# Adding the residual rows by accumulating DMAs instead of on VectorE in three of four column blocks

## The chip, the cores and the metric

The kernel runs on one core of a Trainium2 chip. The metric is the device time of one execution in microseconds (us). The core has TensorE (PE, matmuls; PEld is its weight load), VectorE (DVE), ScalarE (ACT), GpSimd (POOL) and SyncE (SP), each with a program of its own and an in-order queue; they wait for one another by semaphores. Sixteen DMA engines move data between the device memory (DRAM), where inputs and outputs lie, and the on-chip buffers.

## The reference

One layer of a diffusion backbone on 512 latent tokens of width 2048 with 256 context tokens. Three head groups (a Hyena long convolution, latent attention with 8 heads, pooling) give a mixed row of 2048 values per token; what ends the layer is this:

```python
x_l = x_l + gt * (out_l @ w_out[l])
return rmsnorm(x_l, final_norm_g)
```

`out_l` is the mixed 512x2048 matrix, `w_out` is 2048x2048, `gt` a gate of one row of 2048 values, `x_l` the layer's input x (the residual), and the norm divides each row by the root of its mean square and multiplies by `final_norm_g`. All of it is float32.

## The kernel before

All engines' programs are written out by hand, one function per engine, with semaphores. This case is about the last stage, the output product. Precision is kept by splitting each operand into a rounded high part and a rest: each product is three matmuls (high times high, high times low, low times high).

The output has 4 column blocks b of 512 columns and 4 token tiles tok of 128 rows; each (b, tok) has a PSUM bank, and bank sets alternate with b. The inner dimension is cut into 4 chunks c, so the stage has 16 chunks n = 4b + c. For a chunk:

- SP loads its weights, 1 MB, to one of three places `wo_raw` (`load_out`, L426), when the chunk three earlier is done on PE.
- ACT rounds them to `wo_hi` (`wo_high`, L850), one of two places, so it waits until PE is done with chunk n - 2.
- DVE takes the difference `wo_lo` (`wo_low`, L1417).
- PE waits for `wo_lo` and runs 48 matmuls of 512 columns (`out_part`, L2004), 12 for each token tile. In the last block, chunks 14 and 15 are run tile by tile (c = 2, then c = 3 for tok 0, and so on).

A block b is finished by the following steps for its 4 token tiles. `residual` on DVE multiplies the PSUM bank by the gate row in place (L1424), waits for that, and adds x, which lies in the row buffer `y`, into `y` (L1426). `row_squares` on ACT (L860) squares 512 columns of `y` and sums them per row. POOL multiplies the same columns by the norm's gain (L506). For blocks 0 to 2 the residuals stand on DVE behind `wo_low(4b+5)`, the squares on ACT behind `wo_high(4b+5)` and ahead of `wo_high(4b+6)`. PE lets block 2 begin when block 0's residuals are done, and block 3 when block 1's are, since they share banks.

After block 3 a tail follows for each token tile: residual, square, the row's sum and root, its reciprocal, scaling of the 2048 columns (1024 by ACT, L1012, and 512 each in two DVE instructions, L1611 and L1612), and two stores of 512 KB by SP. ACT and DVE wait there for POOL's gain products of block 2 (`gained`).

SP loads x into the row buffer `y` ahead of the stage: four DMAs of 1 MB (L438) and one of 1 MB for the gain (L439), behind the last attention product. ACT's place around the squares is this:

```python
for n in range(3, 16):
    wo_high(n)
    if n % 4 == 1 and n > 4:
        for tok in range(4):
            row_squares(n // 4 - 1, tok)
```

Of the kernel before, what the change touches and what calls it, by code (L numbers as in the profile page):

```python
# [17 lines left out]
ALU = mybir.AluOpType  # L18
# [3 lines left out]
P = 128  # L22
D = 2048
KT = D // P
L = 512
# [36 lines left out]
def backbone(nc, mem, t, out):  # L62
# [6 lines left out]
    with ExitStack() as ctx:  # L69
# [3 lines left out]
        def sem(name):  # L73
            return ctx.enter_context(nc.semaphore(name))
# [68 lines left out]
        gate_rows_, gain, y_out = at("gate_rows", FREE + 10, D), at("gain", TAB + 10, D), at("y", FREE + 21, 4 * D)  # L143
# [8 lines left out]
        def wa_raw(s):  # L152
            return wa_raw_[:, s * AW:(s + 1) * AW]

        def lane(x, s, n=1024, pitch=1024):
            return x[:, s * pitch:s * pitch + n]
# [72 lines left out]
        def q_square(i):  # L229
# [53 lines left out]
        pool_done, pool_mm, pool_out = sem("pool_done"), sem("pool_mm"), sem("pool_out")  # L283
        rope_step, st_max, st_rec = sem("dve_step_a"), sem("st_max"), sem("st_rec")

        xr_in, gain_in = sem("x_rows_in"), sem("gain_in")
        wo_in = [sem(f"wo_in{s}") for s in range(3)]
        mix_hi, mix_lo, diag_done, gate_mm, gate_out = sem("mix_hi"), sem("mix_lo"), sem("diag_done"), sem("gate_rows_mm"), sem("gate_out")
        wo_hi, wo_lo, wo_mm, mm_done = sem("wo_hi_done"), sem("wo_lo_done"), sem("wo_mm"), sem("wo_bank_mm")
        oscaled, res_done, osq_done, fin_done, stored = (sem("out_scaled"), sem("y_done_o"), sem("sq_done_o"),  # L290
                                                                     sem("fin_done"), sem("stored"))
# [26 lines left out]
        def _(eng):  # L318
# [116 lines left out]
            load_out(3)  # L435
            eng.wait_ge(pv_mm, 8)
            for i in range(4):
                eng.dma_start(y_out[:, i * D:(i + 1) * D], t["x"][i * P:(i + 1) * P, :]).then_inc(xr_in, 16)  # L438
            eng.dma_start(gain[:], t["gain"].to_broadcast([P, D])).then_inc(gain_in, 16)  # L439
            for n in range(4, 16):  # L440
                out_chunk_done(eng, n - 3)
                load_out(n)
# [7 lines left out]
        @block.gpsimd  # L450
        def _(eng):
            steps = [0]

            def link(ins):
                steps[0] += 1
                ins.then_inc(pool_step, 1)
                eng.wait_ge(pool_step, steps[0])

            for j in range(KT):
                s = j % 2  # L460
                eng.wait_ge(wa_hi_done, j + 1)
                if j >= 2:
                    eng.wait_ge(mmA_done, j - 1)
                eng.tensor_tensor(lane(wa_lo, s, AW, AW), wa_raw(s), lane(wa_hi, s, AW, AW), ALU.subtract).then_inc(wa_lo_done, 1)
            for o in range(2):
                for l in range(4):
                    eng.wait_ge(taps_sq, 4 * o + l + 1)
                    a, b = squares[:, 0:L], squares[:, L:2 * L]
                    if l == 0:
                        if o:  # L470
                            eng.wait_ge(norm_mm, 1)
                        eng.tensor_tensor(total, a, b, ALU.add).then_inc(sq_sum, 1)
                    else:
                        link(eng.tensor_tensor(a, a, b, ALU.add))
                        eng.tensor_tensor(total, total, a, ALU.add).then_inc(sq_sum, 1)
                        eng.wait_ge(sq_sum, 4 * o + l + 1)

            eng.wait_ge(rope_in, 80)
            for g in range(4):
                eng.wait_ge(ev_done, 27 + g)  # L480
                half = 1 << g
                x = U[:, (T_POOL + g) * L:(T_POOL + g + 1) * L]
                if g == 0:
                    link(eng.memset(pads[0], 0.0))
                link(eng.tensor_copy(pads[0][:, 8:8 + L], x))
                a, n = pads[0], 528
                for d in range(g + 1):
                    b = pads[1 + d % 2]
                    n -= 1 << d
                    link(eng.tensor_tensor(b[:, 0:n], a[:, 0:n], a[:, (1 << d):(1 << d) + n], ALU.add))  # L490
                    a = b
                s = a[:, 8 - half:8 - half + L]
                link(eng.tensor_tensor(s[:, 0:8], s[:, 0:8], edge[:, 16 * g:16 * g + 8], ALU.mult))
                link(eng.tensor_tensor(s[:, L - 8:L], s[:, L - 8:L], edge[:, 16 * g + 8:16 * g + 16], ALU.mult))
                link(eng.tensor_scalar(s, s, 1.0 / (2 * half), 1.0, ALU.mult, ALU.mult))
                eng.tensor_tensor(x, s, x, ALU.subtract).then_inc(pool_done, 1)
                eng.wait_ge(pool_done, g + 1)


            eng.wait_ge(gain_in, 16)  # L500
            for b in range(3):
                for tok in range(4):
                    n = 4 * b + tok
                    eng.wait_ge(osq_done, n + 1)
                    yy = y_out[:, tok * D + b * L:tok * D + (b + 1) * L]
                    eng.tensor_tensor(yy, yy, gain[:, b * L:(b + 1) * L], ALU.mult).then_inc(gained, 1)  # L506

        @block.scalar
        def _(eng):
# [341 lines left out]

            def row_squares(b, tok):
                n = 4 * b + tok
                eng.wait_ge(res_done, n + 1)
                if n:
                    eng.wait_ge(osq_done, n)
                else:

                    eng.wait_ge(gate_mm, 16)
                eng.activation(out_tmp[:], y_out[:, tok * D + b * L:tok * D + (b + 1) * L], ACT.Square,  # L860
                               accum_out=ss[:, 4 * tok + b:4 * tok + b + 1]).then_inc(osq_done, 1)
# [89 lines left out]
            for n in range(34):  # L951
                p, i = n // 8, n % 8
# [47 lines left out]
# [6 lines that stand above are left out]
                row_squares(3, tok)  # L1006
                eng.wait_ge(row_sum, tok + 1)
                eng.activation(rs[:, 2 * tok:2 * tok + 1], rs[:, 2 * tok:2 * tok + 1], ACT.Sqrt, bias=eps[:, 0:1], scale=1.0 / D).then_inc(root_done, 1)
                eng.wait_ge(row_scale, tok + 1)
                eng.wait_ge(gained, 9 + tok)  # L1010
                yy = y_out[:, tok * D:tok * D + 1024]
                eng.activation(yy, yy, ACT.Copy, scale=rs[:, 2 * tok + 1:2 * tok + 2]).then_inc(fin_act, 1)  # L1012

        @block.vector
        def _(eng):
# [403 lines left out]
            def residual(b, tok):  # L1419
                n = 4 * b + tok  # L1420
                eng.wait_ge(mm_done, n + 1)
                yy = y_out[:, tok * D + b * L:tok * D + (b + 1) * L]
                bank = psum[:, 4 * (b % 2) + tok, :]
                eng.tensor_tensor(bank, bank, gate_rows_[:, b * L:(b + 1) * L], ALU.mult).then_inc(oscaled, 1)  # L1424
                eng.wait_ge(oscaled, n + 1)
                eng.tensor_tensor(yy, bank, yy, ALU.add).then_inc(res_done, 1)  # L1426
# [104 lines left out]
            for n in range(34):  # L1531
                p, i = n // 8, n % 8
# [58 lines left out]
            eng.wait_ge(gate_mm, 16)  # L1591
            eng.tensor_copy(gate_rows_[:].rearrange("p (a b) -> p a b", a=4), psum[:, 4:8, :]).then_inc(gate_out, 1)
            eng.wait_ge(gate_out, 1)
            eng.wait_ge(xr_in, 64)
            for n in range(4, 16):
                wo_low(n)
                if n % 4 == 1 and n > 4:
                    for tok in range(4):
                        residual(n // 4 - 1, tok)
            eng.wait_ge(gain_in, 16)  # L1600
            for tok in range(4):
                residual(3, tok)
                eng.wait_ge(osq_done, 13 + tok)
# [11 lines left out]
        def _(eng):  # L1615
# [392 lines left out]
            def out_chunk(b, c):  # L2008
                for tok in range(4):
                    mm = out_part(b, c, tok)  # L2010
                    if c == 3:
                        mm.then_inc(mm_done, 1)
                if c < 3:
                    mm.then_inc(wo_mm, 1)
# [7 lines left out]
            for n in range(34):  # L2022
                p, i = n // 8, n % 8
# [49 lines left out]
            eng.wait_ge(gate_out, 1)  # L2073
            for b in (1, 2):
                if b == 2:
                    eng.wait_ge(res_done, 4)
                for c in range(4):
                    out_chunk(b, c)
            eng.wait_ge(res_done, 8)
            out_chunk(3, 0)  # L2080
            out_chunk(3, 1)

# [8 lines left out]
def build(nc, t, out):  # L2091
    with ExitStack() as ctx:
        def alloc(name, cols):
            return ctx.enter_context(nc.sbuf_tensor(name, [P, cols], F32))

        mem = {n: alloc(n, c) for n, c in (("par", N_PAR), ("gcol", 16), ("ident", P), ("ones", P), ("eps", 1))}
        base = (nc.sbuf_base + 31) // 32 * 32

        def at(name, tile, cols, dt=F32):

            return nc.alloc_sbuf_tensor_at(name, [P, cols], dt, offset=base + int(tile * 2048))

        mem["at"], mem["UG"], mem["U"] = at, alloc("UG", KT * L), alloc("U", U_COLS)
        backbone(nc, mem, t, out)
# [106 lines left out]
```

## Time and profile before

| | us |
|---|---|
| median of 3 executions | 993.85 (992.87 to 996.38) |
| the profiled execution | 992.26 |
| its span, first to last instruction | 990.5 |
| mean granted TensorE clock | 0.992 of full speed |
| PE busy | 952.0 (96% of the span) |
| DVE busy | 620.5 (63%) |
| ACT busy | 397.6 (40%) |
| POOL busy | 95.9 (10%) |

Each row of the profile names the line of the kernel, the engine, the operation, the output and the inputs with their shapes. A time in a timeline counts from the span's start. In square brackets stands how long the engine was idle ahead of the instruction, and whose instruction ended that. Ends of matmuls are modelled and overlap: their starts tell the pace. The output stage is the last 185 us or so of the span.

### The profile page before, as it was taken

What the parts mean: (1) busy time and instruction counts of PE and PEld (TensorE: products, weight loads), DVE (VectorE), ACT (ScalarE), POOL (GpSimd) and SP (SyncE); (2) the same over time, 40 slices, a digit from 0 to 9 for tenths busy, and PEclk for the clock granted to TensorE, in tenths of its full rate; (3) what the DMA queues carried; (4) which work ended last, traced back from release to release, by engine and by line L of the source; (5) the groups of instructions that cost most, each with busy time, mean ns of one, the idle gap of its engine ahead of it and who ended that gap; (6) DMA issues with size and microseconds to landing.
All of it is one profiled execution on the core that took longest, in us unless ns stands there. A gap on an engine that the chain in (4) does not pass through costs nothing.

```text
span 990.5 us, 12597 instructions
## 1 busy us (share of the span) xinstructions
PE 952.0 (96%) x5074; PEld 788.2 (80%) x5074; DVE 620.5 (63%) x817; ACT 397.6 (40%) x622; POOL 95.9 (10%) x77
## 2 busy tenths in 40 slices
PE   5999998899999999999999999999999999999996
PEld 3677786678888789888888888888888888888875
DVE  2676987777765676736785563767776765413234
ACT  3555665355224433222322422645445451213124
POOL 1222200210002200000003360000000000202020
PEclk9999999989999999999999999999999999999998
DMA  9999922222222222248784223101002126222314
GB/s 369 426 424 390 333 86 75 85 65 65 85 85 85 75 64 65 78 171 297 255 302 144 86 85 128 43 12 43 12 1 85 44 80 260 85 85 91 122 43 170
DMA packets 28550, 136.17 MB, mean 137 GB/s; under 512 B 3563, under 2 KB 4011, under 8 KB 21452
## 3 DMA queue, kind: packets, MB, share of 16 engines
q1 hardware_dynamic: 28060, 135.23, 38.1%
q8 instruction: 40, 0.66, 0.3%
q10 hardware_dynamic: 432, 0.13, 0.1%
q14 instruction: 18, 0.15, 0.0%
HBM read 131.16 MB, written 4.19 MB: 137 GB/s over the span
## 4 chain that ended last, share of the span: by engine, by line
PE 78%; DVE 11%; ACT 4%; DMA 4%; issue 2%; SPq 0%; DVEq 0%; ACTq 0%
PE pp L1698 31%; PE pp L2004 17%; PE pp L1728 17%; PE pp L1645 4%; DMA wa_raw<-in_wa_dram 2%; PE pp L1622 2%; PE pp L1967 2%; PE pp L1649 1%; DVE w_lo L1127 1%; DVE pt_lo L1397 1%; DMA ada_raw<-in_w_ada_dram 1%; PE pp L1959 1%; PE pp L1958 1%; DVE softmax_stats L1382 1%; ACT U L819 0%
## 5 line engine op out<-in xcount | busy, mean ns | idle before, releaser
L1698 PE MATMUL pp<-h_hi,w_hi 128*128 128x512 f32 x544 | 216.0, 397 | 8.2 <-ACT UG L616 6.2
L1698 PE MATMUL pp<-h_lo,w_hi 128*128 128x512 f32 x544 | 213.1, 392 | 0.0
L1698 PE MATMUL pp<-h_hi,w_lo 128*128 128x512 f32 x544 | 212.9, 391 | 0.0
L1127 DVE TENSOR_TENSOR w_lo<-w_raw,w_hi 128x1024 fp32r<-128x1024 f32 x68 | 86.5, 1272 | 101.0 <-ACT w_hi L612 100.7
L612 ACT ACTIVATE w_hi<-w_raw 128x1024 fp32r<-128x1024 f32 x68 | 71.9, 1058 | 171.2 <-PE pp L1698 133.4
L1698 PEld LDWEIGHTS pp<-h_hi,w_hi 128*128 128x128 f32 x544 | 102.9, 189 | 33.5 <-issue 9.1
L1698 PEld LDWEIGHTS pp<-h_hi,w_lo 128*128 128x128 f32 x544 | 102.8, 189 | 22.0
L1698 PEld LDWEIGHTS pp<-h_lo,w_hi 128*128 128x128 f32 x544 | 103.1, 189 | 21.2 <-issue 0.7
L2004 PE MATMUL pp<-wo_hi,m_hi 128*128 128x512 f32 x256 | 100.7, 393 | 1.7 <-DVE wo_lo L1417 1.7
L2004 PE MATMUL pp<-wo_hi,m_lo 128*128 128x512 f32 x256 | 99.6, 389 | 0.0
L2004 PE MATMUL pp<-wo_lo,m_hi 128*128 128x512 f32 x256 | 99.6, 389 | 0.0
L1417 DVE TENSOR_TENSOR wo_lo<-wo_raw,wo_hi 128x2048 fp32r<-128x2048 f32 x16 | 36.7, 2291 | 84.1 <-ACT wo_hi L850 84.0
L850 ACT ACTIVATE wo_hi<-wo_raw 128x2048 fp32r<-128x2048 f32 x16 | 30.6, 1914 | 93.0 <-PE pp L2004 93.0
L2004 PEld LDWEIGHTS pp<-wo_hi,m_hi 128*128 128x128 f32 x256 | 48.1, 188 | 12.4 <-DVE wo_lo L1417 2.1
L2004 PEld LDWEIGHTS pp<-wo_lo,m_hi 128*128 128x128 f32 x256 | 48.1, 188 | 10.2 <-issue 0.5
L2004 PEld LDWEIGHTS pp<-wo_hi,m_lo 128*128 128x128 f32 x256 | 48.1, 188 | 10.1
L506 POOL TENSOR_TENSOR y<-y,gain 128x512 f32<-128x512 f32 x12 | 15.5, 1296 | 345.9 <-ACT out_tmp L860 345.6
L1397 DVE TENSOR_TENSOR pt_lo<-pp,pt_hi 128x768 fp32r<-128x768 f32 x32 | 30.5, 953 | 26.1 <-ACT pt_hi L827 26.0
L827 ACT ACTIVATE pt_hi<-pp 128x768 fp32r<-128x768 f32 x32 | 26.0, 812 | 50.9 <-PE pp L1967 50.9
L1622 PE MATMUL pp<-ada_raw,silu_spread 128*32 128x256 f32 x512 | 33.8, 406 | 8.2 <-DMA ada_raw<-in_w_ada_dram 7.8
L819 ACT ACTIVATE U<-pp,softmax_stats 128x768 f32<-128x768 f32 x32 | 28.9, 903 | 27.8 <-DVE softmax_stats L1384 27.6
L1645 PE MATMUL pp<-a_hi,wa_hi 128*128 128x512 f32 x80 | 35.3, 441 | 2.5 <-DVE a_lo L1031 2.5
(308 smaller groups left out, 1876.3 us busy)
## 6 DMA issues: line engine op xcount, KB each, us to landing
w_raw<-in_wb_dram SPq DMA_DIRECT2D x68, 512.0 KB, 3.6
ada_raw<-in_w_ada_dram SPq DMA_DIRECT2D x15, 2048.0 KB, 12.8
w_gate_raw<-in_w_gate_dram SPq DMA_DIRECT2D x16, 1024.0 KB, 4.9
wo_raw<-in_w_out_dram SPq DMA_DIRECT2D x16, 1024.0 KB, 4.8
wa_raw<-in_wa_dram SPq DMA_DIRECT2D x16, 320.0 KB, 7.6
UG<-in_xT_dram SPq DMA_DIRECT2D x8, 512.0 KB, 8.7
y<-in_x_dram SPq DMA_DIRECT2D x4, 1024.0 KB, 9.3
out_dram<-y SPq DMA_DIRECT2D x8, 512.0 KB, 3.2
```

Source lines behind the costliest of these rows:

```text
L612: eng.activation(lane(wb_hi, n % 2), lane(wb_raw, n % KW), ACT.Copy).then_inc(wb_hi_done, 1)
L819: eng.activation(prob(n % 3).rearrange("p (a b) -> p a b", a=2), psum[:, 2 * (n % 2):2 * (n % 2) + 2, 0:384], ACT.Exp, bias=st[:, 4 * s + ...
L827: eng.activation(pt_hi[:].rearrange("p (k q) -> p k q", k=6)[:, :, o:o + P], psum[:, 4:6, :].rearrange("p a b -> p (a b)")[:, 0:LK].rearra ...
L850: eng.activation(wo_high_[n % 2][:], wo_raw[n % 3][:], ACT.Copy).then_inc(wo_hi, 1)
L1127: eng.tensor_tensor(lane(wb_lo, n % KW), lane(wb_raw, n % KW), lane(wb_hi, n % 2), ALU.subtract).then_inc(wb_lo_done, 1)
L1397: eng.tensor_tensor(lo, psum[:, 4:6, :].rearrange("p a b -> p (a b)")[:, 0:LK].rearrange("p (k q) -> p k q", k=6), hi, ALU.subtract).then_ ...
L1417: eng.tensor_tensor(wo_low_[n % 3][:], wo_raw[n % 3][:], wo_high_[n % 2][:], ALU.subtract).then_inc(wo_lo, 1)
L1622: mm = eng.matmul(ps[7][32 * strip:32 * strip + 32, 0:256], spread[:, 32 * kk:32 * kk + 32], src[:, kk * 256:(kk + 1) * 256], start=kk < 4 ...
L1645: mm = eng.matmul(ps[i][:], w, x, start=first and n == 0, stop=last and n == 2)
L1698: mm = eng.matmul(ps[i][:], w, x, start=(kk == 0 and m == 0), stop=(kk == KT - 1 and m == 2))
L1728: mm = eng.matmul(dst, w, x, start=first and m == 0, stop=last and m == 2)
L2004: mm = eng.matmul(psum[:, 4 * (b % 2) + tok, :], a, v[:, w:w + L], start=(kk == 0 and m == 0), stop=(kk == 15 and m == 2))
```

## The change

In blocks 0 to 2 DVE writes the gated product straight from PSUM to `y` and adds nothing. GpSimd then issues a DMA for each (b, tok) that reads 128x512 values (256 KB) of x from DRAM and adds them onto `y`. These are the first DMAs in POOL's program. ACT's squares of block b wait until all four DMAs of that block have landed (semaphore `xacc_in` at 64b + 64); before, square (b, tok) waited for the add of its own tile. PE lets blocks 2 and 3 begin when the gated products of blocks 0 and 1 are there. SP loads only the last 512 columns of x ahead (4 DMAs of 256 KB in place of 4 of 1 MB), and the loads of x and of the gain share one semaphore. Block 3 keeps its residual on DVE.

```diff
@@ SP
-                eng.dma_start(y_out[:, i * D:(i + 1) * D], t["x"][i * P:(i + 1) * P, :]).then_inc(xr_in, 16)
-            eng.dma_start(gain[:], t["gain"].to_broadcast([P, D])).then_inc(gain_in, 16)
+                eng.dma_start(y_out[:, i * D + 1536:(i + 1) * D], t["x"][i * P:(i + 1) * P, 1536:D]).then_inc(xr_in, 16)
+            eng.dma_start(gain[:], t["gain"].to_broadcast([P, D])).then_inc(xr_in, 16)
@@ POOL
-            eng.wait_ge(gain_in, 16)
+            def residual_rows(b, tok):
+                n = 4 * b + tok
+                eng.wait_ge(oscaled, n + 1)
+                eng.dma_start(y_out[:, tok * D + b * L:tok * D + (b + 1) * L], t["x"][tok * P:(tok + 1) * P, b * L:(b + 1) * L],
+                              accum_op=ALU.add).then_inc(xacc_in, 16)
+
+            for tok in range(4):
+                residual_rows(0, tok)
+            eng.wait_ge(xr_in, 80)
             for b in range(3):
                 for tok in range(4):
                     n = 4 * b + tok
                     eng.wait_ge(osq_done, n + 1)
                     yy = y_out[:, tok * D + b * L:tok * D + (b + 1) * L]
                     eng.tensor_tensor(yy, yy, gain[:, b * L:(b + 1) * L], ALU.mult).then_inc(gained, 1)
+                if b < 2:
+                    for tok in range(4):
+                        residual_rows(b + 1, tok)
@@ ACT, row_squares
-                eng.wait_ge(res_done, n + 1)
+                if b < 3:
+                    eng.wait_ge(xacc_in, 64 * b + 64)
+                else:
+                    eng.wait_ge(res_done, tok + 1)
@@ DVE, residual
+                if b < 3:
+                    eng.tensor_tensor(yy, bank, gate_rows_[:, b * L:(b + 1) * L], ALU.mult).then_inc(oscaled, 1)
+                    return
                 eng.tensor_tensor(bank, bank, gate_rows_[:, b * L:(b + 1) * L], ALU.mult).then_inc(oscaled, 1)
                 eng.wait_ge(oscaled, n + 1)
                 eng.tensor_tensor(yy, bank, yy, ALU.add).then_inc(res_done, 1)
@@ DVE, around the stage
-            eng.wait_ge(xr_in, 64)
...
-            eng.wait_ge(gain_in, 16)
+            eng.wait_ge(xr_in, 80)
@@ PE
                 if b == 2:
-                    eng.wait_ge(res_done, 4)
+                    eng.wait_ge(oscaled, 4)
...
-            eng.wait_ge(res_done, 8)
+            eng.wait_ge(oscaled, 8)
```

Two places show what stands in a row on an engine. In the rows below, the number behind a name (`wo_hi_137`) is a buffer, the semaphores that a row waits for stand in brackets, and x3 is three equal rows. `out_scaled` is the semaphore of the gated products, `y_done_o` that of the adds, `sq_done_o` that of the squares, `x_rows_added` that of the new DMAs.

POOL from the end of its pooling work to the end of its program, before:

```order
L493 TENSOR_TENSOR U<-U,edge 128x8 [waits pool_step_p]
L494 TENSOR_TENSOR U<-U,edge 128x8 [waits pool_step_p]
L495 TENSOR_SCALAR U<-U 128x512 [waits pool_step_p]
L496 TENSOR_TENSOR U<-U 128x512 [waits pool_step_p]
L506 TENSOR_TENSOR y<-y,gain 128x512 [waits sq_done_o,gain_in,pool_done]
L506 TENSOR_TENSOR y<-y,gain 128x512 [waits sq_done_o] x11
```

POOL at the same place, after:

```order
L497 TENSOR_TENSOR U<-U 128x512 [waits pool_step_p]
L505 DMA y<-in_x_dram 128x512 [waits out_scaled,pool_done]
L505 DMA y<-in_x_dram 128x512 [waits out_scaled] x3
L516 TENSOR_TENSOR y<-y,gain 128x512 [waits sq_done_o,x_rows_in]
L516 TENSOR_TENSOR y<-y,gain 128x512 [waits sq_done_o] x3
L505 DMA y<-in_x_dram 128x512 [waits out_scaled] x4
L516 TENSOR_TENSOR y<-y,gain 128x512 [waits sq_done_o] x4
```

Four DMA issues now stand ahead of each block's four gain products, and the products of a block stand ahead of the next block's issues (block 2 repeats the last two rows).

ACT from the high part of chunk 5 to that of chunk 7, before:

```order
L850 ACTIVATE wo_hi_138<-wo_raw_133 128x2048 [waits wo_bank_mm,wo_in2]
L860 ACTIVATE out_tmp,row_sums<-y 128x512 [waits gate_rows_mm,y_done_o]
L860 ACTIVATE out_tmp,row_sums<-y 128x512 [waits sq_done_o,y_done_o] x3
L850 ACTIVATE wo_hi_137<-wo_raw_131 128x2048 [waits wo_mm,wo_in0]
L850 ACTIVATE wo_hi_138<-wo_raw_132 128x2048 [waits wo_mm,wo_in1]
```

ACT at the same place, after:

```order
L863 ACTIVATE wo_hi_138<-wo_raw_133 128x2048 [waits wo_bank_mm,wo_in2]
L876 ACTIVATE out_tmp,row_sums<-y 128x512 [waits gate_rows_mm,x_rows_added]
L876 ACTIVATE out_tmp,row_sums<-y 128x512 [waits sq_done_o,x_rows_added] x3
L863 ACTIVATE wo_hi_137<-wo_raw_131 128x2048 [waits wo_mm,wo_in0]
L863 ACTIVATE wo_hi_138<-wo_raw_132 128x2048 [waits wo_mm,wo_in1]
```

No instruction has moved on ACT; the four squares now wait for DMAs, and the high part of chunk 6 (`wo_hi_137` in the fourth row) stands behind them. On DVE the 12 adds of blocks 0 to 2 are gone.

## Rows read from the trace of the kernel before

**Rows 1.** The page, part 1: busy time, share of the span and instructions.

```profile
PE 952.0 (96%) x5074; PEld 788.2 (80%) x5074; DVE 620.5 (63%) x817; ACT 397.6 (40%) x622; POOL 95.9 (10%) x77
```

**Rows 2.** Windows: stretch, length; PE, PEld, DVE, ACT, POOL busy; clock; DMA share; GB/s.

```profile
849.60:860.50 10.90, 10.90 (x50) 9.02 (x49) 7.49 (x9) 4.81 (x9) 4.31 (x4) 1.00 0.27 97
860.50:871.40 10.90, 10.90 (x50) 9.03 (x49) 2.29 (x1) 1.92 (x2) 0.84 (x1) 1.00 0.29 98
```

**Rows 3.** Waits from 838 us on: engine, line, releaser: us in total, times, longest.

```profile
DVE wo_lo L1417 <- ACT wo_hi L850: 78.2, 11, 8.6
ACT wo_hi L850 <- PE pp L2004: 77.0, 11, 12.6
...
PE pp L2004 <- DVE wo_lo L1417: 1.7, 1, 1.7
```

**Rows 4.** Timeline of DVE around block 0's residuals: start, us, instruction.

```profile
853.80 0.69 DVE L1424 TENSOR_TENSOR pp<-pp,gate_rows 128x512 f32<-128x512 f32 x1
854.52 0.69 DVE L1426 TENSOR_TENSOR y<-pp,y 128x512 f32<-128x512 f32 x1
855.13 0.69 DVE L1424 TENSOR_TENSOR pp<-pp,gate_rows 128x512 f32<-128x512 f32 x1
...
862.47 2.29 DVE L1417 TENSOR_TENSOR wo_lo<-wo_raw,wo_hi 128x2048 fp32r<-128x2048 f32 x1 [3.26 <-ACT wo_hi L850]
```

**Rows 5.** Timeline of ACT: the first square of block 0, the next high parts.

```profile
855.25 0.63 ACT L860 ACTIVATE out_tmp<-y 128x512 f32<-128x512 f32 x1 [3.69 <-DVE y L1426]
855.79 0.19 ACT L860 ACTIVATION_READ_ACCUMULATOR out_tmp<-y 128x1 f32 x1
...
860.52 1.92 ACT L850 ACTIVATE wo_hi<-wo_raw 128x2048 fp32r<-128x2048 f32 x1 [0.55 <-PE pp L2004]
871.40 1.92 ACT L850 ACTIVATE wo_hi<-wo_raw 128x2048 fp32r<-128x2048 f32 x1 [8.96 <-PE pp L2004]
```

**Rows 6.** Timeline of PE where chunk 5 ends and chunk 6 begins.

```profile
871.37 0.39 PE L2004 MATMUL pp<-wo_lo,m_hi 128*128 128x512 f32 x1
```

**Rows 7.** Timeline of POOL: gain products of blocks 0 and 2.

```profile
856.14 5.20 POOL L506 TENSOR_TENSOR y<-y,gain 128x512 f32<-128x512 f32 x4 [269.18 <-ACT out_tmp L860]
...
943.09 5.29 POOL L506 TENSOR_TENSOR y<-y,gain 128x512 f32<-128x512 f32 x4 [38.23 <-ACT out_tmp L860]
```

**Rows 8.** Costliest POOL groups of 128x512: xcount, busy us, mean ns, idle before.

```profile
L475 POOL TENSOR_TENSOR temps<-temps,z_spec 128x512 f32<-128x512 f32 x6 | 11.0, 1832 | 0.5
```

**Rows 9.** DMA issues of L410 (8 of 256 KB, 4 of 768 KB) and their landing.

```profile
L410 SPq DMA_DIRECT2D wh_raw<-in_w_heads_dram x12: 327/328/432, 593.8 to 698.0; - x12
...
DMA to landing us min/median/max: 2.6/3.3/5.1
```

**Rows 10.** DMA issues of L438, four of 1 MB in a row.

```profile
L438 SPq DMA_DIRECT2D y<-in_x_dram x4: 328/432/766, 813.3 to 814.7; - x4
...
DMA to landing us min/median/max: 4.8/9.3/12.2
```

**Rows 11.** Timeline of DVE and of POOL where two-input work runs on both.

```profile
186.61 1.78 DVE L1147 SCALAR_TENSOR_TENSOR U<-UG,par,U 128x511 f32<-128x511 f32 x1
188.43 1.66 DVE L1149 SCALAR_TENSOR_TENSOR U<-UG,par,U 128x511 f32<-128x511 f32 x1
190.01 0.74 DVE L1147 SCALAR_TENSOR_TENSOR U<-UG,par,U 128x511 f32<-128x511 f32 x1
...
186.46 1.39 POOL L474 TENSOR_TENSOR z_spec<-z_spec 128x512 f32<-128x512 f32 x1 [5.70 <-ACT z_spec L697]
187.93 1.61 POOL L475 TENSOR_TENSOR temps<-temps,z_spec 128x512 f32<-128x512 f32 x1
```

**Rows 12.** Chain that ended last, in order of time, in block 3.

```profile
958.44 1.93 ACT wo_hi L850
...
962.73 19.35 PE pp L2004 x84
```

**Rows 13.** Timeline of ACT: the first scaling in the tail.

```profile
969.88 1.16 ACT L1012 ACTIVATE y<-y,row_scale 128x1024 f32<-128x1024 f32 x1 [0.23 <-DVE row_scale L1607]
```

More of the change, by code:

```diff
@@ L284, in backbone @@
         rope_step, st_max, st_rec = sem("dve_step_a"), sem("st_max"), sem("st_rec")
-        xr_in, gain_in = sem("x_rows_in"), sem("gain_in")
+        xr_in, xacc_in = sem("x_rows_in"), sem("x_rows_added")
         wo_in = [sem(f"wo_in{s}") for s in range(3)]
```

## The prediction

> **What bounds the kernel now.** I read the busy times first: PE is busy for 952 of 990.5 us, DVE for 63%, POOL for 10% [rows 1]. That says that work taken off DVE is worth something only where PE waits for DVE. So I read the output stage chunk by chunk: in the stretch with block 0's residuals and in the one behind it PE is busy for 10.90 of 10.90 us at full clock, though DVE has 7.49 us of work in the first and 2.29 in the second [rows 2]. The list of waits from 838 us on says the same: DVE waits for ACT and ACT for PE, 77 to 78 us in total each, and PE waits for DVE once, for 1.7 us [rows 3]. That one wait is in block 3, at 961 to 962.7 us, for the low part of chunk 15 [rows 12], which the change leaves alone. PE's matmuls set the pace everywhere that the change touches.
>
> **What it removes.** Twelve adds of 0.69 us on DVE [rows 4], 8.3 us of DVE time; with the wait between multiply and add, a block's residuals shrink from some 5.4 to 2.5 us. All of it lies beside running matmuls, and no engine on the path waits for it: worth 0. SP's loads of x ahead shrink from 4 MB to 1 MB; they began at 813.3 us and landed after 4.8 to 12.2 us [rows 10], when PE did not wait for a DMA: 0. PE's gates for blocks 2 and 3 open some 3 us earlier, but in block 0 before they opened near 859 us and block 2 begins four chunks of 10.88 us after 849.6, near 893: 0. The tail of block 3 is unchanged instruction for instruction: 0. The gain of the change is thus bounded by 0 from above, as long as nothing of PE's is shortened.
>
> **What it adds, and its cover.** The new wait is in front of ACT's four squares, and queued behind them on ACT is the high part of chunk 6 (of chunks 10 and 14 in the other blocks); DVE's low part waits for that, and PE for the low part. I work it out for block 0 and call T the time at which ACT's first square can start, that is when all four DMAs have landed.
>
> The latest T that costs nothing: the first matmul of chunk 6 is at 871.37 us [rows 6], and I allow 0.2 us ahead of it for the load of its weights (788.2 us for 5074 loads is 0.16 each [rows 1]), so the low part must be there by 871.2. From the start of the high part to the end of the low part it is 860.52 to 862.47 + 2.29 = 864.76, that is 4.24 us [rows 4, 5]. A square with its accumulator read takes 855.25 to 855.98, 0.73 us [rows 5], four in a row 3.0 us. So the low part ends at T + 3.0 + 4.24 = T + 7.24, and T may be 863.9.
>
> One more cost is moved with the squares: POOL's four gain products follow the squares, 1.3 us each [rows 7]. They start at T + 0.75 and end at T + 5.95, and DVE's low part starts at T + 4.95. Before, they ended at 861.34 and the low part began at 862.47, so they never met. Where DVE and POOL work with two inputs from SBUF side by side, the same DVE form took 1.78 and 1.66 us in place of 0.74, and POOL 1.61 in place of 1.3 [rows 7, 11]: about 0.65 us more on DVE for each us of overlap. For 1.0 us of overlap that is 0.7 us (bounds 0 and 1.0), and T may be 863.9 - 0.7 = 863.2. The Trainium skill's page "SBUF — State Buffer" (Who interferes with whom) says that a DVE instruction with two SBUF inputs contends with a GpSimd instruction that reads SBUF; the rows agree, and by its absence T could be 863.9.
>
> When T comes: the products follow each other on DVE at 0.61 us, so the first is done at 853.80 + 0.69 = 854.5 and the last at 856.3 [rows 4]. No DMA of POOL and no accumulating DMA is in this trace, so I bound both costs. **Issue on POOL, g each:** at least what SP needs, 0.33 us [rows 9]; at most POOL's slowest group on this shape, 1.83 us [rows 8]. I take the middle, 1.1: it writes no tile, but it is software on the same engine. **Landing behind the issue:** for loads of 256 and 768 KB 2.6, 3.3 and 5.1 us (least, median, most) [rows 9]; an adding DMA moves the destination too, 512 KB in all, within these sizes; I take 3.3. Then T = 854.5 + 4 x 1.1 + 3.3 = 862.2. The ends are max(854.5 + 1.3, 856.3 + 0.3) + 2.6 = 859.2 and 854.5 + 7.3 + 5.1 = 866.9. The SP loads of weights are issued at 849.6 and 860.5 and keep the DMA engines busy for 0.27 to 0.29 of a chunk [rows 2], so there is room between them. The skill's page "DMA: Bandwidth & Descriptors" (Anatomy of one DMA; Latency and other measured facts) gives about 1 us to the first byte on GpSimd's path and 2.0 us plus bytes over 436 GB/s for a transfer; an estimate from it is T = 854.5 + 4 + 2.6 = 861.1, no other verdict; no row here shows it.
>
> At T = 862.2 the low part of chunk 6 is done at 862.2 + 7.24 + 0.7 = 870.1 us, 1.1 us ahead of PE's need. The new path is hidden, by a cover of 6.4 us (864.76 to 871.2) of which 5.3 us are used up. Blocks 1 and 2 have the same geometry 43.5 and 87.0 us later.
>
> **What it costs when the cover is gone.** For T later than 863.2, PE stalls d = T - 863.2 ahead of chunks 6, 10 and 14. In block 2 part of it is given back: PE waits 1.7 us for chunk 15's low part there already [rows 12], and ACT can do that high part right behind the late one, so only d - 1.65 is left. The sum is 2d + max(0, d - 1.65). Latest end: d = 3.7, 7.4 + 2.05 = 9.5 us. POOL's products of block 2 then end at about 866.9 + 6 + 87 = 960 us or some us later, and ACT needs them at 969.9 [rows 7, 13]: still hidden.
>
> **The sum.** The profiled execution takes 992.26 us, 990.5 span and 1.8 around it. Removed on the path 0, added 0: 992.26 again. The median of the three runs stands 1.6 us above that execution, so the forecast on their scale is 993.9 us.
>
> **Rivals.**
> - Issues on POOL are slow (slower than before). POOL is software, and its 128x512 instructions take 1.3 to 1.8 us [rows 7, 8]. At g = 1.83 and 3.3 for landing T = 865.1, d = 1.9, and the sum is 3.8 + 0.25 = 4.1 us: 998.0. It decides from g = 1.35 on (854.5 + 4g + 3.3 = 863.2). For it: nothing in the trace shows a DMA built by POOL. Against: SP and POOL need no data pass for an issue. Chance 0.23.
> - The adding transfers are slow: they read the destination, add and write it back. Four DMAs in a row moved 4 MB in 12.2 us [rows 10], some 340 GB/s; at a quarter of that rate for the 1 MB of a block it is 12 us from the first issue's end at 855.6, T = 867.6, d = 4.4, and the sum is 8.8 + 2.75 = 11.5 us: 1005.4; at a third 9.3 us, T = 864.9 and 3.5 us. The middle of the two is 1001. Chance 0.14.
> - Only the meeting of POOL and DVE bites: T is near 862.2, and the low part is slowed by more than the 1.8 us left without the slowing. That would need an overlap of 2.7 us at 0.65; 994.5 or so. Chance 0.04.
> - It gets faster. The one mechanism would be PE waiting for DVE in blocks 0 to 2, and no row has that [rows 3]. What is left is a lighter DMA load around 813 us. 990 to 992. Chance 0.04.
> - The change doesn't take the adds off DVE: excluded, the 12 adds are gone in its program.
>
> **How the numbers follow.** Hidden: 0.55, at 993.9. A measurement of this kernel can tell about 0.3% (3 us) from no change. Within 3 us: hidden and the third rival, 0.59. Slower by more: 0.23 + 0.14 = 0.37. Faster: 0.04. The range starts at 992.4, a little under the lowest of the three runs (992.87); upwards it takes in the slow issues and most of the slow transfers, up to 1003. Left out are about 0.04 below, 0.06 above, and some 0.1 for costs that no row bounds.
>
> **What would show it in the profile after.** (1) PE's stretches 849.6 to 882 are full as before, and there are no waits of PE for the low part except the 1.7 us one. (2) POOL's issues of block 0 follow each other at 1.1 us from 854.5 on. (3) ACT's first square of block 0 starts at 862.2, the four are back to back within 3 us, each released by a DMA. (4) The high part of chunk 6 starts near 865.2 instead of 860.5, the low part ends near 870, slowed to some 3 us. A first square later than 863.2 makes the prediction wrong, by 2 to 3 us of stall for each us. A first issue on POOL with a cost of its own would show in block 0 alone.

## The result

| | before | after |
|---|---|---|
| median, us (14 executions each) | 994.02 (992.06 to 996.38) | 1000.1 (995.05 to 1006.34) |
| the profiled execution, us | 992.26 | 1002.13 |
| its span, us | 990.5 | 1000.3 |
| mean granted TensorE clock in it | 0.992 | 0.986 |
| first high part of block 1 (chunk 5) on ACT to the last residual on DVE, us | 849.64 to 982.11: 132.5 | 855.06 to 992.00: 136.9 |

The changed kernel is slower: ratio 1.0062, interval 1.0042 to 1.0082. The likeliest case of the prediction (hidden, 993.9) didn't come; the range (992.4 to 1003) holds the median, through one of the rivals.

The last line of the table is the stage that the change touches, and it is 4.5 us longer. The other 5.4 us by which the profiled execution is longer lie before it, in code that the change leaves alone (PE's first matmul on `wo_hi` starts at 800.94 us and not at 795.54); the starts of this stage in the profiled executions of this study lie anywhere from 849.4 to 855.1 us (852.70 in one that is the kernel before up to there). So executions are compared here by the stage, and kernels by ratios of many executions.

Here are parts 1 and 3 of the page after (part 3 lists the DMA queues: packets, MB, the time of the packets as a share of 16 engines' span). DVE has lost its 12 adds [rows 1]; the new queue moves 3.15 MB in 2.0% of the engines' time:

```profile
PE 956.9 (96%) x5074; PEld 790.4 (79%) x5074; DVE 614.8 (61%) x805; ACT 397.6 (40%) x622; POOL 105.5 (11%) x89
...
q1 hardware_dynamic: 28060, 132.09, 37.0%
q0 software_dynamic: 1728, 3.15, 2.0%
```

These are the waits after, from 838 us on. The first, second and last answer to the three of [rows 3], the third is new:

```profile
DVE wo_lo L1433 <- ACT wo_hi L863: 89.4, 10, 14.3
ACT wo_hi L863 <- PE pp L2022: 66.1, 9, 12.6
ACT out_tmp L876 <- DMA y<-in_x_dram: 40.1, 3, 14.1
...
PE pp L2022 <- DVE wo_lo L1433: 5.1, 3, 2.4
```

PE now waits three times for a low part. The chain that ended last shows the way there in block 0 (start, us, what). Before, this stretch of the chain was matmuls without a break [rows 2]:

```profile
859.30 1.21 DVE y L1441 x2
860.51 0.03 issue
860.54 1.86 POOL y L505 x2
862.40 8.61 DMA y<-in_x_dram
871.03 0.73 ACT out_tmp L876 x2
...
874.20 1.82 ACT wo_hi L863
876.02 0.02 issue
876.04 3.06 DVE wo_lo L1433
879.10 0.04 issue
879.15 22.09 PE pp L2022 x96
```

The order is product, issue, 8.6 us of DMA, squares, high part, low part, and only then chunk 6. The 8.6 us count from the start of the fourth issue (862.40); that issue itself ends at 864.25. The timelines of PE (the first matmuls of chunks 6, 10 and 14) give the waits one by one, in brackets behind each:

```profile
879.15 0.50 PE L2022 MATMUL pp<-wo_hi,m_hi 128*128 128x512 f32 x1 [2.42 <-DVE wo_lo L1433]
...
924.42 0.50 PE L2022 MATMUL pp<-wo_hi,m_hi 128*128 128x512 f32 x1 [1.44 <-DVE wo_lo L1433]
...
969.51 0.50 PE L2022 MATMUL pp<-wo_hi,m_hi 128*128 128x512 f32 x1 [1.27 <-DVE wo_lo L1433]
```

The wait for chunk 15's low part [rows 3, 12] is gone in turn: the stall ahead of chunk 14 covers it.

### The profile page after: what moved, and what is told of

It is laid out like the page before. It is cut to its first block, busy times and chain, and to the rows that moved or that the text cites. A ratio compares the mean times of both kernels' runs of the same rounds, so it can differ in the third digit from the quotient of the medians.

```text
span 1000.3 us, 12598 instructions
## 1 busy us (share of the span) xinstructions
PE 956.9 (96%) x5074; PEld 790.4 (79%) x5074; DVE 614.8 (61%) x805; ACT 397.6 (40%) x622; POOL 105.5 (11%) x89
## 3 DMA queue, kind: packets, MB, share of 16 engines
q0 software_dynamic: 1728, 3.15, 2.0%
## 4 chain that ended last, share of the span: by engine, by line
PE 69%; DVE 14%; DMA 8%; ACT 5%; issue 3%; SPq 0%; POOL 0%; DVEq 0%; ACTq 0%
PE pp L1716 26%; PE pp L1746 17%; PE pp L2022 13%; PE pp L1663 3%; DMA wa_raw<-in_wa_dram 2%; DMA w_raw<-in_wb_dram 2%; PE pp L1640 2%; DMA y<-in_x_dram 2%; PE pp L1985 2%; DVE wo_lo L1433 2%; DMA ada_raw<-in_w_ada_dram 1%; DVE w_lo L1143 1%; PE pp L1667 1%; DVE gate_acc L1154 1%; ACT wo_hi L863 1%
## 5 line engine op out<-in xcount | busy, mean ns | idle before, releaser
L2022 PEld LDWEIGHTS pp<-wo_lo,m_hi 128*128 128x128 f32 x256 | 48.1, 188 | 10.2 <-issue 0.5
L505 POOL DMA_DIRECT2D y<-in_x_dram x12 | 10.8, 1343 | 327.2 <-DVE y L1441 327.2
```

The costliest lines, as they stand in the source:

```text
L2022: mm = eng.matmul(psum[:, 4 * (b % 2) + tok, :], a, v[:, w:w + L], start=(kk == 0 and m == 0), stop=(kk == 15 and m == 2))
```

## The experiments

Every ratio is to the kernel before, run on the same chip beside it. "Stage" is the stretch of the table above. Some edits change who waits for what, some change the DMAs themselves, and the others ask what else the change could cost and what a PE wait is worth.

**The changed kernel again** (no edit).

> The changed kernel as it is. The profile after shows three PE waits for the low part (chunks 6, 10, 14) and an output stage (start of chunk 4 to PE's last matmul) that is 4.5 us longer than before, while the median was 6.1 us longer and the runs spread over 11 us. If the stage is the whole cost, the ratio is near 1.0045; if something of the new queue acts elsewhere too, it stays at 1.006 or more and the spread stays wide.

Ratio 1.0055 (1.0034 to 1.0076), median 999.32 to 993.16. The stage of its profiled execution took 141.0 us, 8.5 more than before, and block 0 shows why. ACT's first square came 14.3 us behind DVE's first product (870.20 and 855.94) instead of 11.8, so PE waited 4.83 us; and behind that wait the granted clock was 0.8 (windows: stretch, length, PE busy, PEclk, DMA share, GB/s):

```profile
872.00:876.00 4.00, 1.44 (x7) 1.00 0.35 98
876.00:880.00 4.00, 1.72 (x4) 0.80 0.41 168
880.00:884.00 4.00, 4.00 (x15) 0.77 0.00 0
884.00:888.00 4.00, 4.00 (x20) 1.00 0.00 0
```

From 880 to 884 us PE is busy all the time, and the window counts 15 matmuls where the next one counts 20. In finer windows the clock is 0.51 from 878.4 to 881.8 us, the lower of its two levels (1.2 GHz), and 0.99 to 1.00 around that. Its price can be read from the restarts of PE: chunk 10 starts 46.8 us behind chunk 6 (878.28 to 925.09) and 45.3 us in the first profile, though PE's wait ahead of it is the same (1.41 and 1.44 us). So the low clock cost 1.5 us, and the other 2.4 us that block 0 cost more are the longer wait (4.83 and 2.42 us). The same code costs 4.5 or 8.5 us, depending on how late a landing is.

The ratio lies between the two answers of the expectation, and the stage alone, at 4.5 to 8.5 us, is enough for the medians' 6.1 us; two profiles can't say what it costs in a typical execution. The spread doesn't decide it either: it was 11.3 us in the first measurement, but 6.0 us here, where the kernel before had 6.0 us as well (992.06 to 998.09).

**The squares one chunk later** (late_squares).

```diff
                 wo_high(n)
-                if n % 4 == 1 and n > 4:
+                if n % 4 == 2 and n > 4:
                     for tok in range(4):
                         row_squares(n // 4 - 1, tok)
```

> ACT's squares of blocks 0 to 2 stand one chunk later, behind the high part of chunk 6 (10, 14) instead of ahead of it; DMAs, products and waits are the same. Theory 'squares ahead of the high part': PE no longer waits for the low part of chunks 6, 10 and 14, the stage is as long as before (132.5 us), and some 4.5 us of the loss are gone. Rival 'the adding DMAs cost by themselves' (they slow the weight loads or something outside the stage): the loss stays at 3 us or more with the squares out of the way.

Ratio 0.9996 (0.9981 to 1.0011); stage 851.11 to 983.58, 132.5 us. The whole loss is gone, with the same twelve DMAs, as slow as before (landing 3.7 / 6.5 / 8.3 us behind the start of the issue: least, median, most). ACT's timeline, where the high part of chunk 6 now comes before the wait:

```profile
861.99 1.92 ACT L863 ACTIVATE wo_hi<-wo_raw 128x2048 fp32r<-128x2048 f32 x1 [8.96 <-PE pp L2022]
866.76 0.63 ACT L876 ACTIVATE out_tmp<-y 128x512 f32<-128x512 f32 x1 [2.85 <-DMA y<-in_x_dram]
```

The rival that the DMAs cost 3 us or more by themselves falls.

**A wait for each tile** (own_waits). Four semaphores, one for each tok; the squares stay where they were. To have enough semaphores, the weight loads of this stage share theirs with loads that are long done.

```diff
-                              accum_op=ALU.add).then_inc(xacc_in, 16)
+                              accum_op=ALU.add).then_inc(xacc_in[tok], 16)
...
-                    eng.wait_ge(xacc_in, 64 * b + 64)
+                    eng.wait_ge(xacc_in[tok], 16 * b + 16)
```

> Each square waits for the adding DMA of its own token tile (four semaphores) instead of for all four. In the profile after the first of four landed 3.9 us and the last 8.6 us behind its issue. Theory 'the last landing decides': the last square starts at the same time, but the three others are done by then, so the high part starts 2.4 us earlier; the stall of 2.4 us ahead of chunks 6 and 10 shrinks to near 0, and 3 to 4.5 us come back. Rival 'each landing is late by a fixed latency': the squares come apart by the pace of the issues (0.9 us), with the same gain; the spacing of the squares tells the two apart: 1.5 us or more for a rate, 0.9 us for issues with a fixed latency.

Ratio 1.0003 (0.9989 to 1.0018); stage 849.60 to 982.18, 132.6 us: all of it comes back. ACT's squares of block 0 each stand behind their own landing:

```profile
858.93 0.63 ACT L876 ACTIVATE out_tmp<-y 128x512 f32<-128x512 f32 x1 [7.41 <-DMA y<-in_x_dram]
...
861.19 0.63 ACT L876 ACTIVATE out_tmp<-y 128x512 f32<-128x512 f32 x1 [1.53 <-DMA y<-in_x_dram]
...
863.17 0.63 ACT L876 ACTIVATE out_tmp<-y 128x512 f32<-128x512 f32 x1 [1.26 <-DMA y<-in_x_dram]
...
866.13 0.63 ACT L876 ACTIVATE out_tmp<-y 128x512 f32<-128x512 f32 x1 [2.24 <-DMA y<-in_x_dram]
```

The spacing is 2.3, 2.0 and 3.0 us, where POOL's four issues took 3.70 us in all. Landings set apart by more than the issues mean a rate. In blocks 1 and 2 the spacing is less even (3.8, 1.3, 1.3 and 2.6, 1.7, 1.2); two gaps of each are 1.2 to 1.7 us, near the 1.5 us that the expectation asks for or below it, but the four squares are spread over 6.3 and 5.5 us, again more than their issues.

In block 0 nothing is left to spare: the low part of chunk 6 ended at 870.99 us, and PE's first weight load of the chunk waited 0.2 us for it (871.04), which the first matmul (871.10) just covered; the matmuls behind it are late by 0.1 us. The low part took 2.29 us and not 3.06, since POOL's products no longer met it. A landing as late as that of after_again would have stalled PE here too.

**Plain DMAs** (plain_dma). In `residual_rows`, `accum_op=ALU.add` is left out, so x takes the place of the gated product in blocks 0 to 2 of the output.

> GpSimd's twelve DMAs write x over the product instead of adding to it (the product is left out of blocks 0 to 2 of the output); bytes, rows, queue, issues and waits are as in the changed kernel. In that kernel a block's 1 MB took about 7 us of the DMA engines, and the last landing came 11 to 14 us behind DVE's first product. Theory 'the adding makes them slow': the last landing comes some 4 us behind the last issue, 8 us behind the first product, no stalls ahead of chunks 6, 10 and 14, ratio near 1.000. Rival 'any DMA of this queue, or rows of 2 KB, are slow': landings and stalls as in the changed kernel, ratio 1.005.

Ratio 0.999 (0.9974 to 1.0006), stage 132.5 us, no stall; the first square of block 0 comes 6.9 us behind the first product, and not 11.8. Three things differ from the adding DMAs: the landing (3.1 / 3.5 / 4.3 us behind the start of the issue, and not 3.8 / 6.5 / 8.6), the issue (2.34 us for four on POOL, and not 3.71) and the engines' time, for the same bytes:

```profile
q0 software_dynamic: 960, 3.15, 0.9%
```

That is 0.9% of 993.5 us against 2.0% of 1000.3: 8.9 and 20.0 us of all sixteen engines, or 3.0 and 6.7 us for a block. Adding makes the engines work 2.2 times as long, in 1728 packets and not 960.

**Half the columns** (half_columns). Each adding DMA takes 256 of the 512 columns; the other half of x is left out.

```diff
-                eng.dma_start(y_out[:, tok * D + b * L:tok * D + (b + 1) * L], t["x"][tok * P:(tok + 1) * P, b * L:(b + 1) * L],
+                eng.dma_start(y_out[:, tok * D + b * L:tok * D + b * L + 256], t["x"][tok * P:(tok + 1) * P, b * L:b * L + 256],
```

> The adding DMAs take 256 of the 512 columns of each tile (half of x is left out of blocks 0 to 2); number of DMAs and of rows unchanged, 128 KB each. Theory 'cost by bytes': the engines' time per block falls from 7 to 3.5 us, the last landing comes 3 us or more earlier, the stalls are gone. Rival 'cost by row (a fixed time for each read, add and write)': engines' time and landings hardly change, and the stalls of 2 to 5 us ahead of chunks 6 and 10 stay.

Ratio 0.9991 (0.9974 to 1.0007), stage 132.5 us, no stall. Landing 3.1 / 4.0 / 4.5 us, the first square 7.7 us behind the first product:

```profile
q0 software_dynamic: 1728, 1.57, 1.1%
```

The same number of packets with half the bytes takes 1.1% and not 2.0%: the cost goes by bytes, with little for each packet. POOL's issues took 3.70 us for four as before, so they alone had not made the squares late.

**The weight load held back** (held_load).

```diff
                 out_chunk_done(eng, n - 3)
+                if n in (7, 11, 15):
+                    eng.wait_ge(xacc_in, 64 * (n // 4))
                 load_out(n)
```

> SyncE holds the load of chunk 7 (11, 15) until the four adding DMAs of the block have landed; before, that load of 1 MB is issued while two or three of them are under way. Theory 'they collide': the last landing comes 1 to 2 us earlier and steadier, the stall ahead of chunks 6 and 10 shrinks from 2.4 us to about 1, ratio 1.002. Rival 'the adding DMAs are slow on their own': landings within 0.5 us of the changed kernel's, ratio 1.005 unchanged.

Ratio 1.002 (1.0005 to 1.0035), stage 849.93 to 985.23, 135.3 us; PE's waits ahead of chunks 6, 10 and 14 are 1.35, 0.85 and 1.20 us. The squares come 10.7, 10.3 and 10.7 us behind the first product, and not 11.8, 10.9 and 10.7. So part of the lateness in block 0 is the 1 MB load that starts while the adding DMAs are under way (and itself lands after 7.3 us instead of 4.8). The larger part of the lateness stays without it. Of the time, more is gone: the ratio is 1.002 here and was 1.0055 and 1.0062. The load may also make the scatter of block 0, but one profile can't show that.

**One DMA for a block** (one_dma).

```diff
+                if tok < 3:
+                    return
+                eng.wait_ge(oscaled, 4 * b + 4)
+                eng.dma_start(y_out[:].rearrange("p (t d) -> p t d", t=4)[:, :, b * L:(b + 1) * L],
+                              t["x"].rearrange("(t p) d -> p t d", t=4)[:, :, b * L:(b + 1) * L],
                               accum_op=ALU.add).then_inc(xacc_in, 16)
...
-                    eng.wait_ge(xacc_in, 64 * b + 64)
+                    eng.wait_ge(xacc_in, 16 * b + 16)
```

> One adding DMA of 1 MB per block, issued when the block's fourth product is there, in place of four of 256 KB. Theory 'the rate of adding sets the landing' (2.2 us of all sixteen engines for 256 KB): the transfer takes the same 7 us, begins some 1.8 us later than the first of the four did, so the squares start 1 to 2 us later than in the changed kernel and the stalls ahead of chunks 6 and 10 grow to 3 to 4 us each, ratio 1.008. Rival 'four issues of software on GpSimd cost': with one issue, 2 to 3 us of issue time fall away, the squares start no later, ratio 1.005 or less.

Ratio 1.0159 (1.0141 to 1.0177), twice the loss expected. The transfer needs hardly less of the engines (1.8% for 3.15 MB) and lands 10.2 to 10.9 us behind its issue; the squares come 13.0 to 14.0 us behind the first product, and PE waits 4.60, 3.54 and 3.92 us. The expected direction was right, the size not. Two things differ from what was expected: the squares come 2 to 3 us later than in the changed kernel and not 1 to 2, and with each wait goes a low clock. Windows at blocks 0 and 1:

```profile
874.00:878.00 4.00, 0.22 (x1) 1.00 0.68 227
878.00:882.00 4.00, 3.18 (x8) 0.57 0.10 39
882.00:886.00 4.00, 4.00 (x19) 1.00 0.00 0
...
926.00:930.00 4.00, 2.39 (x6) 0.54 0.53 219
930.00:934.00 4.00, 4.00 (x13) 0.61 0.00 0
```

The stage took 148.8 us (852.55 to 1001.39), 16.4 more than before, of which PE's waits are 12.1. In finer windows the clock is 0.50 in three stretches: 878.5 to 881.9, 926.3 to 933.1 and 977.5 to 980.9 us. Each begins before PE has restarted (878.82, 927.61 and 977.91).

**GpSimd's queue in the kernel before** (before_pool_queue). The 32 KB table of the pooling's edges is loaded by GpSimd and not by SyncE, with a semaphore of its own (freed as above).

```diff
-                    for dst, name in ((rope_c, "rope_c"), (rope_s, "rope_s"), (swap[:], "swap"), (wp[:], "w_pool"), (edge[:], "edge")):
+                    for dst, name in ((rope_c, "rope_c"), (rope_s, "rope_s"), (swap[:], "swap"), (wp[:], "w_pool")):
...
-            eng.wait_ge(rope_in, 80)
+            eng.wait_ge(y_done, 12)
+            eng.dma_start(edge[:], t["edge"]).then_inc(edge_in, 16)
+            eng.wait_ge(edge_in, 16)
```

> The kernel before, with one small plain DMA (32 KB, the table of the pooling's edges) issued by GpSimd instead of SyncE; nothing else uses GpSimd's queue. Theory 'the queue's mere presence costs': slower than before by 1 to 2 us, with the spread of the changed kernel. Rival 'presence is free': within 1 us of before, spread as before.

Ratio 1.0005 (0.9991 to 1.0019), spread 992.85 to 997.64. One small DMA of that queue costs nothing that can be measured; for the twelve adding ones late_squares says the same.

**A tile ahead in block 3, in the kernel before and with late squares** (before_tiles_ahead, late_and_tiles).

```diff
+            out_part(3, 2, 0)
+            out_part(3, 2, 1)
             for tok in range(4):
-                out_part(3, 2, tok)
                 out_part(3, 3, tok).then_inc(mm_done, 1)
+                if tok < 2:
+                    out_part(3, 2, tok + 2)
```

> The kernel before, with one edit on PE in block 3: the part of chunk 14 for the second token tile comes ahead of chunk 15's part for the first, and so on, always one tile ahead. The one wait of PE for a low part in the stage is 1.67 us, ahead of chunk 15. Theory 'a PE wait in this stage costs the end its full length': the wait is gone and the span is 1.6 to 1.7 us shorter, ratio 0.998. Rival 'the tail of the last token tile sets the end': the wait is gone, the end stays.

> The changed kernel with the squares one chunk later and, on PE, chunk 14's part of each next tile ahead of chunk 15's part of this one: both edits that took a wait of PE away. From the kernel before with the second edit alone (ratio 0.9985), the adding DMAs should give nothing more: stage 131.8 us, ratio 0.998 to 0.999. If the 8 us of DVE work taken off in blocks 0 to 2 were worth something, it would be below that.

PE's wait for chunk 15's low part is gone in both. The ratio is 0.9985 (0.9972 to 0.9999) in the first, 1.0002 (0.999 to 1.0014) in the second; the stages are 131.77 and 131.78 us. So each gives back 0.7 us and not 1.67: DVE's last two residuals now come 4.0 us apart and not 5.4, and the last has no idle time of DVE ahead of it (983.81 is the third tile's last instruction):

```profile
980.48 0.70 DVE L1424 TENSOR_TENSOR pp<-pp,gate_rows 128x512 f32<-128x512 f32 x1 [1.36 <-PE pp L2004]
...
983.81 0.75 DVE L1612 SCALAR_TENSOR_TENSOR y<-y,row_scale,gain 128x512 f32<-128x512 f32 x1
984.47 0.69 DVE L1424 TENSOR_TENSOR pp<-pp,gate_rows 128x512 f32<-128x512 f32 x1
```

The third tile's tail, a chain between DVE and ACT, has become what the last tile waits for. On PE itself the wait of 1.67 us is worth 2.0: in before_tiles_ahead PE's last matmul starts 130.1 us behind the start of the stage, and 132.0 us in the kernel before. And 8 us of DVE work less (late_and_tiles) adds nothing to the 0.7 us. Whether either version is really faster than the kernel before, the medians can't tell; the first one's interval ends just below 1, and the second missed the 0.998 to 0.999 that was expected, though its interval holds 0.999.

## Why the prediction was right or wrong

- **What bounds, and the value of what is removed: right.** With the landings out of the way (late_squares, own_waits) the stage is 132.5 us, as before. Taking 12 adds off DVE was worth 0.
- **The latest T that costs nothing, and what comes of a later one: right, but for one matmul.** The squares of block 0 began at 871.03 in a stage that had begun 5.4 us later than before; on the scale of before that is T = 865.6, and d = 865.6 - 863.2 = 2.4 us. PE waited 2.42. The low part beside POOL's last product took 3.06 us instead of 2.29: 0.8 for the 0.7 assumed (for 0.9 us of overlap, so about 0.85 us for each us and not 0.65). Four squares took 3.1 us for 3.0.
- **The matmul that was misread.** The matmul at 871.37 us [rows 6] is the second of chunk 6. Each group of three begins with high times high, as the restarts above show, and that one stands at 871.14 in the timeline of before. So T could be 863.0 and d was 2.6 us, which is by how much chunk 6 was late: 879.15 - 5.42 - 871.14 = 2.6.

```profile
871.14 0.39 PE L2004 MATMUL pp<-wo_hi,m_hi 128*128 128x512 f32 x1
871.37 0.39 PE L2004 MATMUL pp<-wo_lo,m_hi 128*128 128x512 f32 x1
```

- **The part given back in block 3: right in kind.** The stretches between the three restarts of PE (879.15, 924.42, 969.51) are 45.3 and 45.1 us instead of four chunks, 43.5; so with the 2.6 of block 0 the shifts are 2.6, 1.8 and 1.6, 5.9 in all (unrounded), of which the stage shows 4.5. 1.4 us came back where the prediction had 1.65. The shifts of blocks 1 and 2 are smaller, since the squares came 10.9 and 10.7 us behind the first product there, and not 11.8; the prediction had one d for all blocks.
- **The issue on POOL: right.** Four took 3.7 us, 0.9 each for the 1.1 assumed. The first began 0.6 us behind its product (860.54 against 859.22 + 0.69), which the sum didn't have. The two differences nearly cancel.
- **The landing: the step that failed.** The prediction took 3.3 us for the landing. Counted as in the profile, from the start of an issue, that held for the first DMA alone (3.9); the four of block 0 landed 3.9, 6.1, 7.1 and 8.6 us behind the starts of their issues. The price in [rows 9] counts from the start as well, but the sum adds it behind the end of the fourth issue. Counted in that way the landing took 6.8 us (864.25 to 871.03), 3.5 more than assumed. The step took a price from loads that were plain, and added it once; but the four share sixteen engines, and adding takes 6.7 us of them for a block (plain: 3.0). T moved by 3.4 us, from 862.2 to 865.6, over a cover that had 1.0 us left (0.8 with the right matmul).
- **The rivals.** The one that came is "the adding transfers are slow", at the higher of its two rates: at a third of 340 GB/s it had T = 864.9 and 3.5 us for the sum, against 865.6 and 4.5. That the median also lies near the 1001 us of this rival is luck: 1001 is the middle between two rates, and what brings the median above the 4.5 us of the first profile is not in the rival. It had a chance of 0.14, less than the slow issue (0.23), which half_columns rules out as the cause: with the issues unchanged the loss is gone. Nothing in the trace of before spoke for the one over the other, but the argument "they read the destination, add and write it back" stood in the text and should have moved the landing in the sum too.
- **What no step had:** the clock behind a long wait of PE, and landings that scatter by 2 to 3 us in block 0. Both are shown for single executions: after_again has a wait 2.4 us longer and a low clock that cost 1.5 us, one_dma three low stretches. They would bring a stage loss of 4.5 us up to the median's 6.1; how many executions of the changed kernel had them is not shown, since only one execution of each measurement is in a trace.

## What to carry to other kernels

Where work was moved from an engine to a DMA here, 0.7 us on the engine gave way to a landing of 4 to 11 us. So look at what stands behind the wait in the waiting engine's queue: one square too early cost 4.5 us, and moving it behind the next urgent instruction cost nothing. Letting each consumer wait for its own transfer cost nothing either, but with nothing to spare in block 0. Cost transfers that are issued in a row by the engines' time for all of them and not by one landing, and take more for adding ones. Where PE is the bound, a wait of some microseconds can cost more than its length (here 1.5 us of low clock behind a wait of 4.8 us).

## What the runs showed of the hardware

- An adding DMA from DRAM onto an on-chip float32 buffer took 2.2 times the DMA engines' time of a plain one of the same bytes and queue (20.0 and 8.9 us of all engines for 3.15 MB), some 157 GB/s; with half the bytes and the same number of packets it took about half.
- Its issue took longer too: four in 3.5 to 3.7 us on POOL, against 2.34 us for four plain ones.
- One adding DMA of 1 MB, issued when the last of four products was ready, let the squares begin 13.0 to 14.0 us behind the start of the first product; four of 256 KB, each issued as its product was ready, 10.6 to 11.8 us in five blocks of the two profiles of the changed kernel and 14.3 in the sixth. A 1 MB load issued meanwhile landed after 6.5 to 7.7 us, and after 4.7 when it was held back.
- With waits of PE of 3.5 to 4.8 us the granted clock fell to its lower level (0.50 to 0.51, 1.2 GHz) for 3.4, 3.4, 3.4 and 6.8 us, in four of four cases. The fall came 0.1 us behind the restart once and before it three times. With waits of 0.9 to 2.4 us the clock stayed at 1.00, in the three of the changed kernel's first profile and the three of held_load.
- The low part (DVE, two inputs, 128x2048) took 3.0 to 3.1 us where its first 0.9 us or so met POOL's last gain product, in the changed kernel, plain_dma and half_columns, and 2.29 us where it met none, as in own_waits and late_squares.
